# Where the sums of squares of an RMS norm are formed: one folded tile inside the ramp, and the residual sum's early part in the last group

## The reference, cut to what matters

```python
def rms_norm(x, g):
    xf = x.astype(jnp.float32)
    y = xf * lax.rsqrt(jnp.mean(xf * xf, axis=-1, keepdims=True) + EPS)
    return (y * g.astype(jnp.float32)).astype(x.dtype)
...
        x = x + rms_norm(out, g[1])
        f, fb = conv_ffn(rms_norm(x, g[2]), ffn_buf0[l], P['w_ffn_g'][l], P['w_ffn_u'][l],
                         P['ffn_conv_w'][l], P['ffn_conv_b'][l], P['w_ffn_d'][l])
        x = x + rms_norm(f, g[3])
```

## Time and profile before

| | |
|---|---|
| median of 3 runs | 2734.64 us (2731.52 to 2736.24) |
| the profiled execution's own time | 2734.95 us |
| its span | 2733.3 us |
| PE busy | 2634.2 us, 96% of the span |
| DVE busy | 1625.8 us, 59% |
| ACT busy | 1113.3 us, 41% |
| POOL busy | 229.5 us, 8% |
| bytes read from HBM | 425.05 MB, 157 GB/s over the span |

### The profile page before, as it was taken

One profiled execution on the slowest core, in us unless ns is written; L12 is line 12 of the kernel. 1 busy time (PEld: TensorE's weight loads), 2 busy tenths in 40 slices (PEclk: granted clock), 3 DMA queues, 4 the chain that ended last, 5 costly groups with the idle time before them and its releaser, 6 DMA issues.

```text
span 2733.3 us, 53926 instructions
## 1 busy us (share of the span) xinstructions
PE 2634.2 (96%) x20517; PEld 2491.4 (91%) x20517; DVE 1625.8 (59%) x2549; ACT 1113.3 (41%) x1603; POOL 229.5 (8%) x281
## 2 busy tenths in 40 slices
PE   6899999999999999998999999998999999999999
PEld 5888999999999999998895557898999999999998
DVE  3889676664666466667641224467665566546665
ACT  3457444433334333445432222344443343333344
POOL 1033210000000000030300000031000000000012
PEclk9999999999999999999989998799999999999999
DMA  5544545555555555554543320154555555555553
GB/s 191 158 143 145 177 150 160 182 181 181 184 178 183 179 183 180 181 180 130 150 137 102 87 70 24 56 184 132 183 178 183 180 181 182 180 184 179 182 180 110
DMA packets 440034, 429.78 MB, mean 157 GB/s; under 512 B 37436, under 2 KB 428692, under 8 KB 439656
## 3 DMA queue, kind: packets, MB, share of 16 engines
q1 hardware_dynamic: 436312, 419.83, 49.1%
q0 software_dynamic: 3200, 6.06, 0.7%
q10 hardware_dynamic: 432, 2.66, 0.3%
HBM read 425.05 MB, written 3.95 MB: 157 GB/s over the span
## 4 chain that ended last, share of the span: by engine, by line
PE 90%; DVE 3%; issue 3%; POOL 2%; ACT 1%; SPq 1%; DMA 0%; POOLq 0%; DVEq 0%; ACTq 0%
PE acc L1603 26%; PE acc L1604 26%; PE acc L1605 26%; PE mis L1889 2%; PE mis L1911 2%; PE acc L1879 1%; PE mis L1641 1%; DVE lo L1059 1%; PE mis L1890 1%; PE mis L1960 1%; PE mis L1959 1%; POOL aa L644 0%; POOL aa L642 0%; PE mis L1978 0%; SPq L521 0%
## 5 line engine op out<-in xcount | busy, mean ns | idle before, releaser
L1603 PE MATMUL acc<-xnh,hi 128*128 128x264 f32 x3664 | 1052.0, 287 | 46.8 <-issue 14.9
L1605 PE MATMUL acc<-xnh,lo 128*128 128x264 f32 x3664 | 1047.0, 286 | 0.0
L1604 PE MATMUL acc<-xnl,hi 128*128 128x264 f32 x3664 | 1046.0, 285 | 0.0
L1059 DVE TENSOR_TENSOR lo<-raw,hi 128x1024 fp32r<-128x1024 f32 x752 | 924.0, 1283 | 165.5 <-ACT hi L718 164.8
L718 ACT ACTIVATE hi<-raw 128x1024 fp32r<-128x1024 f32 x752 | 756.7, 1049 | 463.5 <-DMA raw<-in_w_ffn_d 248.6
L1603 PEld LDWEIGHTS acc<-xnh,hi 128*128 128x128 f32 x3664 | 698.8, 191 | 51.3 <-issue 41.5
L1604 PEld LDWEIGHTS acc<-xnl,hi 128*128 128x128 f32 x3664 | 699.6, 191 | 0.3
L1605 PEld LDWEIGHTS acc<-xnh,lo 128*128 128x128 f32 x3664 | 697.1, 190 | 0.0
L1603 PE MATMUL acc<-hh,hi 128*128 128x264 f32 x2112 | 600.5, 284 | 0.0
L1605 PE MATMUL acc<-hh,lo 128*128 128x264 f32 x2112 | 599.4, 284 | 0.0
L1604 PE MATMUL acc<-hl,hi 128*128 128x264 f32 x2112 | 598.5, 283 | 0.0
(11 more groups left out here) (300 smaller groups left out, 2275.7 us busy)
## 6 DMA issues: line engine op xcount, KB each, us to landing
raw<-in_w_ffn_g SPq DMA_DIRECT2D x192, 512.0 KB, 3.5
raw<-in_w_ffn_u SPq DMA_DIRECT2D x192, 512.0 KB, 3.5
raw<-in_w_ffn_d SPq DMA_DIRECT2D x192, 512.0 KB, 3.5
raw<-in_w_rg_in SPq DMA_DIRECT2D x64, 512.0 KB, 3.7
raw<-in_w_rg_o SPq DMA_DIRECT2D x32, 512.0 KB, 3.6
cpage<-in_cache_kv_latent SPq DMA_DIRECT2D x64, 256.0 KB, 2.5
raw<-in_w_mla_o SPq DMA_DIRECT2D x32, 512.0 KB, 3.5
raw<-in_w_dkv SPq DMA_DIRECT2D x8, 512.0 KB, 3.8
```

The costliest lines, as they stand in the source:

```text
L1059: dve.tensor_tensor(lo[:, c % SPLIT, :, 0:n], raw[:, c % RAW, :, 0:n], hi[:, c % SPLIT, :, 0:n].bitcast(F32), ALU.subtract).then_inc(s.lo_ ...
L1603: pe.matmul(out, wh, xh, start=start, stop=False)
L1604: pe.matmul(out, wh, xl, start=False, stop=False)
L1605: return pe.matmul(out, wl, xh, start=False, stop=stop)
```

## The change

In the ramp, DVE folds all 16 squares into tile 8 in five steps (`fold`), the last three of them after the low part of tile 15. PE makes one `row_sum` of that tile, ahead of the matmuls of kk = 14, in place of eight at two places behind them. In the residual norm, PE's two sums over `sq_sum` move ahead of the last chunk of the last group (`early_sum`). For b = 0 and 2, ACT squares the last tile straight from PSUM and DVE's copy of that tile waits for it. In `block_norm` on DVE, the first addition to `x` moves ahead of the second scaling.

```diff
+FOLDS = 5
...
+            def block_norm(b, n_f, acc_done, rows_first=(), c_last=None):
+
+                act.wait_ge(s.acc_read, acc_done - 1)
+                act.activation(sq_last[:, 0, :], f[:, KT - 2, :], ACT.Square).then_inc(s.sq_last, 1)
+                if c_last:
+                    act.wait_ge(s.chunk_used, c_last)
+                    last = acc[(acc_done - 1) % 4][:, 0:T]
+                else:
+                    act.wait_ge(s.acc_read, acc_done)
+                    last = f[:, KT - 1, :]
+                act.activation(sq_last[:, 1, :], last, ACT.Square).then_inc(s.sq_last, 1)
...
-            block_norm(0, N_RGO, 2 * G_FFN0)
+            block_norm(0, N_RGO, 2 * G_FFN0, c_last=C_FFN0)
...
+            def fold(r, sq, n):
+
+                squares, dst, src = ((8, 0, 4), (12, 8, 0), (16, 8, 12), (16, 8, 10), (16, 8, 9))[n]
+                w = min(4, src - dst) if src > dst else 4
+                dve.wait_ge(s.sq_ramp, 16 * r + squares)
+                if n:
+                    dve.wait_ge(s.sq_part, FOLDS * r + n)
+                dve.tensor_tensor(sq[:, dst:dst + w, :], sq[:, dst:dst + w, :], sq[:, src:src + w, :], ALU.add)\
...
                 if j == 9:
-                    square_sums(r, sq, 0)
+                    fold(r, sq, 0)
...
                 if j == 13:
-                    dve.wait_ge(s.sq_part, 2 * r + 1)
-                    square_sums(r, sq, 1)
+                    fold(r, sq, 1)
+                if j == KT - 1:
+                    for n in range(2, FOLDS):
+                        fold(r, sq, n)
...
                     if m:
-                        dve.wait_ge(s.chunk_used, c0 + 32)
+                        dve.wait_ge(s.sq_last, 2 * b + 2)
...
-                    if n + 1 < len(BATCHES) and BATCHES[n + 1][1] <= 8:
+                    if 0 < n and BATCHES[n + 1:] and BATCHES[n + 1][1] <= 8:
                         scaled_f(*BATCHES[n + 1])
                     add_x(u, v)
-                    if n + 1 < len(BATCHES) and BATCHES[n + 1][1] > 8:
+                    if n == 0:
+                        scaled_f(*BATCHES[1])
+                    elif n + 1 < len(BATCHES) and BATCHES[n + 1][1] > 8:
...
+            def early_sum(b, n):
+
+                pe.wait_ge(s.rms_ready, n)
+                pe.wait_ge(s.sq_step, SQ_STEPS * (b + 1))
+                for m in range(2):
+                    row_sum(sq_sum[:, m, :], m == 0, False)
...
+                    if tail and q == n - 1:
+                        early_sum(*tail)
...
+                    if kk == KT - 2:
+                        if n:
+                            pe.wait_ge(s.rms_ready, n)
+                        pe.wait_ge(s.sq_part, FOLDS * (r + 1))
+                        row_sum(sq[:, 8, :], True, True)
...
-                    if kk == 14:
-                        for t in range(8, 14):
-                            ramp_sum(r, n, sq, t)
-                for t in range(14, KT):
-                    ramp_sum(r, n, sq, t)
```

More of the change, by code:

```diff
@@ L1042, in _ @@
             last_down(2, PT_NORM + 5 * KT, C_MO, C_FFN1 + 4)
-            block_norm(2, N_MO, 2 * G_FFN1)
+            block_norm(2, N_MO, 2 * G_FFN1, c_last=C_FFN1)
             ramp(3, PT_NORM + 6 * KT, 48, f, C_FFN1, lambda: scale_pair(2, PT_NORM + 5 * KT, KT // 2 - 1))
@@ L1605, in mm3, with row_sum, group @@
                 return pe.matmul(out, wl, xh, start=False, stop=stop)
-            def group(c, n, g, xh, xl, ready, g_off=0, c_off=0, tiles=2, between=None, tail=False):
+            def row_sum(tile, start, stop):
+                last = pe.matmul(mis[3][:, 0:T], ones[:, :], tile, start=start, stop=stop)
+                if stop:
+                    last.then_inc(s.stat_ready, 1)
+            def early_sum(b, n):
[3 more added lines that the diff above has]
+                    row_sum(sq_sum[:, m, :], m == 0, False)
+            def group(c, n, g, xh, xl, ready, g_off=0, c_off=0, tiles=2, between=None, tail=None):
                 if isinstance(g_off, int):
@@ L1629, in group, with stream @@
                     last.then_inc(s.chunk_used, 1)
-            def stream(c0, g0, xh, xl, ready, tail=False):
+            def stream(c0, g0, xh, xl, ready, tail=None):
                 with pe.Fori(0, 3 if tail else 4) as i:
@@ L1636, in stream @@
                     for a in range(2):
[L1637 to L1653, removed]
+                        group(c0 + 24 + 4 * a, 4, g0 + 6 + a, xh, xl, ready, tail=tail if a else None)
             def ramp(c0, g0, xbase, r, n, sq):
@@ L1671, in ramp, with norm_sum @@
                             last.then_inc(s.chunk_used, 1)
-                    if kk == 14:
-                        for t in range(8, 14):
-                            ramp_sum(r, n, sq, t)
-                for t in range(14, KT):
-                    ramp_sum(r, n, sq, t)
[L1678 to L1683, removed]
+            def norm_sum(b):
                 for m in range(2):
@@ L1754, in _, with ffn @@
                 gelu_pair(3, a, following=False)
-            stream(C_RGO, G_RGO, hh, hl, lambda q: pe.wait_ge(s.h_ready, 4 * (q + 1)), tail=True)
-            def ffn(c00, g00, h0, xbase, r, n_x):
+            stream(C_RGO, G_RGO, hh, hl, lambda q: pe.wait_ge(s.h_ready, 4 * (q + 1)), tail=(0, N_RGO))
+            def ffn(c00, g00, h0, xbase, r, n_x, tail):
                 for sec in range(SECTIONS):
@@ L1765, in ffn @@
                     stream(c0 + 64, g0 + 16, hh, hl, lambda q: pe.wait_ge(s.h_ready, 16 * sec + h0 + 4 * (q + 1)),
[L1766 to L1770, removed]
+                           tail=tail if sec == SECTIONS - 1 else None)
+            norm_sum(0)
+            ffn(C_FFN0, G_FFN0, H_FFN0, XN_1, 1, N_X1, (1, N_F0))
+            norm_sum(1)
             ramp(C_DKV, G_DKV, XN_KV, 2, N_X2, f)
@@ L1999, in _ @@
             pe.wait_ge(s.o_ready, H - 1)
-            stream(C_MO, G_MO, hh, hl, lambda q: pe.wait_ge(s.o_ready, 4 * (q + 1)), tail=True)
-            norm_sum(2, N_MO)
-            ffn(C_FFN1, G_FFN1, H_FFN1, XN_3, 3, N_X3)
+            stream(C_MO, G_MO, hh, hl, lambda q: pe.wait_ge(s.o_ready, 4 * (q + 1)), tail=(2, N_MO))
+            norm_sum(2)
+            ffn(C_FFN1, G_FFN1, H_FFN1, XN_3, 3, N_X3, (3, N_F1))
             pe.wait_ge(s.tail_saved, 56)
@@ L2005, in _ @@
                 turn_out(n)
-            norm_sum(3, N_F1)
+            norm_sum(3)
             for n in range(len(mid) + 2, len(plan)):
```

4 lines of the change are left out of this document (removed).

## The result

The change takes 2715.78 us in the median of 6 runs (2706.44 to 2721.06), beside 2733.55 us (2731.52 to 2736.28, 6 runs) for the kernel before: a ratio of 0.9936, 95% interval [0.9922, 0.9949]. It is 0.6% faster, with an interval that excludes no change, and inside the range of 2705 to 2719; 2710.5 us had been forecast. The profiled execution took 2719.08 us with a span of 2717.4 us.

What follows compares the result with a forecast made beforehand. PE, busy 96% of the span, was taken to bound the kernel, with uncovered chains at ramp ends. 2734.95 - 21.8 (ramps) - 5.3 (clock) + 0.5 (clock at the `lo` gap) + 2.1 (residual) = 2710.45, forecast 2710.5 us, range 2705 to 2719.

Steps and rivals of the forecast that it cites:

- The ramps: At the four ramps' ends, one earlier sum puts root and reciprocal beside matmuls; saves 21.8 us in all.
- the gap for `lo`: Behind ramp 0, PE's second gap, waiting for DVE's `lo`, grows from 3.62 to some 5.4 us.
- The clock behind the ramps: Behind ramps 1, 2 and 3, shorter gaps no longer bring slow matmuls at half clock; saves 5.3 us.
- A gap of 2.2 us followed by a clock of 1.00: Earlier in the trace; taken as evidence that gaps of 0.6 and 1.5 us behind ramps bring no slow clock.
- The residual part: At the residual norms, fourth sums come 0.28, 0.75 and 0.28 us later; with the additions' waits, a cost of 2.1 us.
- The addition's wait on DVE: In the residual norm, the first addition waits for the scaling ahead; costs 0.19 us at each of four norms, 0.76.
- The wait that costs DVE nothing: Rival, 5%: waits in the four additions and the folds cost DVE nothing; 2709 us.
- The slow stretches behind the ramps: Rival, 16%: the clock falls anyway behind ramps 1, 2 and 3, giving 2716 us.
- The residual part was not dearer: Rival, 10%: residual norm changes cost more than forecast, up to 2715 us.
- The later wait for weights: Rival, 5%: the weights' stream sets the pace, so PE waits for chunks and the gain is given back; 2734 us.
- The fold that would hold PE's stream: Rival, 4%: ahead of kk = 14, late DVE folds stall PE; slower from 8.1 us late, 2741 at ten.
- the last term: In the sum, the median of the runs lying 0.3 lower than the profiled execution; left out.

Runs made afterwards that it cites:

- e1: The change with only its ramp part (folds and one sum), the residual norm as in the kernel before: 2720.11 us, ratio 0.9943 to the kernel before.
- e4: The kernel before with four overwritten sums (1.78 us of PE work) added ahead of the attention stage: 2744.12 us, ratio 1.0032.
- e2: The change with only its residual norm part, the ramps as in the kernel before: 2736.91 us, ratio 1.0029 to the kernel before.
- e6: The change with the ramp's one sum ahead of kk = 15 in place of kk = 14: 2713.53 us, ratio 0.9943 to the kernel before.
- e5: The change run again unaltered, on a second chip: 2720.97 us, ratio 0.9963 to the kernel before.
- e9: The change with eight overwritten sums (3.56 us) added ahead of the attention stage: 2712.66 us, ratio 0.9939 to the kernel before.

## Why the prediction was right

- **The ramps.** Forecast 6.0, 5.6, 4.4 and 5.8 us, measured 6.02, 5.45, 4.46 and 5.63: 21.6 of 21.8. The mechanism was the one named: root and reciprocal now lie beside matmuls, and e1 shows that this part alone gives it. Some 3.1 us of ramp 1's gain are the seven sums that PE no longer makes (at the forecast's 0.445 each), and 2.95 the smaller gap, less the wait of 0.36 for the fold. Behind ramp 0 the gap for `lo` grew to 5.12 us, 5.4 forecast.
- **The clock behind the ramps.** Forecast 5.3 us. Behind ramps 2 and 3 it is 1.55 and 1.14 in the table; behind ramp 1 it is 2.54 (821.57 to e1's 819.03, without the residual part): 5.2 in all. (The 1.14 is the least certain: the same part of e1, with a clock of 1.00 behind ramp 3, took 834.8 us, as long as before.) That the two agree so well is luck, since the 5.3 were read from one execution of the kernel before. e4 has the same ramp 1 and the same gap behind it, and there the clock stayed at 1.00 (its gap, then the stretch from it on):

```profile
420.96 0.39 PE L1603 MATMUL acc<-xnh,hi 128*128 128x264 f32 x1 [3.29 <-DVE gs L1327]
```

```profile
421.00:426.60 5.60, 5.60 (x46) 5.60 (x47) 5.60 (x11) 1.30 (x2) 1.01 (x1) 1.00 0.18 54
```

That is 46 matmuls where the earlier trace rows has 25, and the part to ramp 2 took 819.04 us in place of 821.57. Behind ramp 3 of e2 it stayed at 1.00 too, again behind a gap of 3.29. So this term is what the change saves in an execution in which the clock falls behind the old ramps, and less in others. The reason given for it failed as well. A gap of 2.2 us followed by a clock of 1.00 (277.40 on) was taken to clear shorter ones; e6 has a low clock behind a gap of 1.85 us at one ramp and none behind the same gap at another. What holds is that gaps of 0.35 to 0.49 us, and of 1.2 and 1.69 us behind ramp 2, were not followed by one in these profiles.

- **The residual part.** Forecast 0.28, 0.75 and 0.28 us for the sums, measured 0.34, 0.84 and 0.34. The addition's wait on DVE costs 0.12 us at a norm (5.10 of PE's idle time ahead of a ramp against 4.98), 0.19 forecast. At the three norms ahead of a ramp that makes 1.9 us, 1.9 forecast; for the fourth addition (0.19) nothing was measured. This part is a loss: the traces of e2 and of the change show it alike, and e1, without it, is 0.96 us shorter at b = 1.
- **The wait that costs DVE nothing.** The Trainium skill's page "VectorE: DVE Perf Modes", section "The DRAIN you can't avoid", would have made this bubble zero: in the case that it measured the semaphore cost nothing extra. It also says that an instruction that nothing holds starts earlier, which agrees with the overlap of 0.08 us in the prediction. With the old order (e1) PE's idle time ahead of a ramp is 4.98 us again, so the wait does cost something here, 0.12 us, if less than the 0.19 forecast.
- **The other rivals.** The slow stretches behind the ramps did not stay; the median is near the 2716 us of that rival by another way. The residual part was not dearer. (That rival's premise was not quite right: the trace of before does have sums between split matmuls, those between kk = 14 and kk = 15, and the price of 0.445 us comes from them.) The later wait for weights is not there: ramp 1's end to ramp 2 got shorter, not longer. The fold that would hold PE's stream costs 0.36 to 0.40 us, far from the 8.1 from which it would decide.
- **What was mis-sized.** The sum put the change's savings against one profiled execution and took the clock of every part that isn't touched as it was there (the last term, "the median of the runs lies 0.3 lower, which I leave out"). Where the times are short the forecast is met: 2710.6 to 2711.3 us in four runs of e5, one of them profiled, with a stage as long as that of before (2710.5 forecast). In the long ones some 10 us are added, and the median of 2715.78 lies between the two. About half of the change's runs are long ones, few of those before. A second, smaller one of the same kind: the clock behind the gap ahead of `lo` and at the stretch 271.55 cost e5 2.9 us over the first profile, where the forecast had 0.5.
- **Luck.** That the median fell inside the range rests on the mix of short and long runs in six executions. On the chip of e5 the same kernel had a median of 2720.97 us, outside the range. The mechanism of the ramps doesn't depend on this; the total does.

What stays open: by what the stage's length comes up short or long in an execution. Shown is that the same kernel has both, that DVE, ACT and POOL do the same in both, and that PE's clock makes the difference. That a shift of 1.78 us sways the odds is shown for the kernel before, by its times on one chip; for the other shifts it is not shown apart from the chip. Why a shift favours one was not found, nor where the shortest runs of before, e6 and e9 save their time.

## What to carry to other kernels

A sum over partitions that PE makes at the end of a phase is paid twice, once as matmuls and once as the chain of root, reciprocal and evacuation behind it: fold on an engine that has room, leave PE one matmul, and put that a few microseconds of matmuls ahead of the phase's end. Look at what the chain then ends with (here PE's wait of 0.36 us and the gap of 0.35 are in balance: by the traces of the ramps, moving the sum lost and moving the folds gave little). A part of a change that only moves sums earlier can lose, if those sums covered another engine's hop; try the parts apart, and compare parts of the trace with the same instructions before a difference of the medians is put down to the edit. A cost read from one execution, as the low clock behind the ramps was, should be looked for in a second one before it is counted as a saving.

## What was not expected of the hardware

- The attention stage, 3533 matmuls and but for residual norm 2 the same work on every engine, took 543.7 to 548.6 us in seven profiled runs and 554.9 to 559.6 us in seven others, at a granted clock of 0.93 and of 0.90 to 0.91.
- With 1.78 us put in ahead of that stage, 7 of 12 runs of the kernel before took over 2740 us, beside 2 of 23 without it on the same chip.
- The low clock behind a gap is not decided by the gap's length alone: 3.3 us behind ramp 1 was followed by 0.50 in the profile of before and by 1.00 in that of e4, and 1.85 us by 0.68 at ramp 1 and by 1.00 at ramp 3 of one execution (e6).
